# A two-layer decoder with routed experts on one core: gathering raw residual rows, a sliced router, and 32-column tiles in mixed passes

## What is computed

```
scores = sigmoid(h @ w_router)                  # 64 experts
sel = scores + router_bias
grp = sel.reshape(N, 8, 8)                      # 8 groups of 8
gscore = sum of the two largest of each group   # the best 4 groups stay
idx = the 6 largest of sel in those groups
w = scores[idx]; w = w / sum(w) * 2.5
routed = sum over idx of w * swiglu(h, w_gate_up[e], w_down[e])
out = routed + swiglu(h, shared_gate_up, shared_down)
```

## Time and profile before

| what | value |
|---|---|
| median of 3 runs | 1378.45 us (1378.06 to 1379.5) |
| the profiled execution's own time | 1383.0 us |
| its span in the profile | 1381.2 us |
| TensorE busy, matmuls | 1176.0 us, 85% of the span |
| VectorE busy | 422.5 us, 31% |
| ScalarE busy | 253.4 us, 18% |
| moved by DMA | 502.24 MB, mean 364 GB/s |
| chain that ended last | PE 46%, SP's queue 26%, DMA 18%, DVE 5% |
| TensorE's mean granted clock | 0.942 of full speed |

### The profile page before, as it was taken

How to read it: one execution, slowest core, us unless ns; L and a number is a source line. 1 busy time by engine, 2 the same in 40 slices (tenths; PEclk the granted TensorE clock), 3 DMA queues, 4 the chain that set the end, 5 groups by cost and what they waited for, 6 DMA issues and landing times.

```text
span 1381.2 us, 17034 instructions
## 1 busy us (share of the span) xinstructions
PE 1176.0 (85%) x6576; PEld 621.2 (45%) x6576; DVE 422.5 (31%) x1026; ACT 253.4 (18%) x572; POOL 0.4 (0%) x5
## 2 busy tenths in 40 slices
PE   6999788999697799769968889899969779967996
PEld 4886367525243333323227467752524333332332
DVE  1397546312111112112132577531211211211213
ACT  1112513111111101111022263311101110110100
POOL 0000000000000000000000000000000000000000
PEclk9999989999899899999988999999989989998998
DMA  9999896779999999999976705677999999999995
GB/s 348 382 407 411 352 395 248 318 277 425 423 423 424 424 424 424 424 423 423 424 297 264 251 31 186 243 323 278 425 422 424 423 423 424 424 424 423 424 424 214
DMA packets 99913, 502.24 MB, mean 364 GB/s; under 512 B 11865, under 2 KB 37366, under 8 KB 44534
## 3 DMA queue, kind: packets, MB, share of 16 engines
q1 hardware_dynamic: 99366, 500.92, 89.2%
q10 hardware_dynamic: 464, 0.20, 0.1%
HBM read 500.04 MB, written 1.05 MB: 363 GB/s over the span
## 4 chain that ended last, share of the span: by engine, by line
PE 46%; SPq 26%; DMA 18%; DVE 5%; issue 3%; ACT 2%; DVEq 0%; ACTq 0%
PE bank L707 39%; SPq L579 24%; DMA w_gu<-in_moe_w_gate_up 7%; DMA xn<-in_moe_w_gate_up 4%; DMA w_gu_x<-in_moe_w_gate_up 4%; PE bank L925 2%; PE bank L1090 2%; DMA ring<-in_ada_w 2%; PE bank L710 2%; SPq L665 2%; DMA ring<-in_a_w_o 1%; PE bank L1071 1%; SPq L639 1%; ACT p_sb L1310 1%; DVE x L1796 0%
## 5 line engine op out<-in xcount | busy, mean ns | idle before, releaser
L707 PE MATMUL bank<-w_gu,ring 128*32 128x512 f32 (+1 forms) x1024 | 356.6, 672 | 60.8 <-DMA w_gu<-in_moe_w_gate_up 55.0
L707 PEld LDWEIGHTS bank<-w_gu,ring 128*32 128x32 f32 (+1 forms) x1024 | 88.5, 132 | 214.2 <-issue 214.2
L707 PE MATMUL bank<-ring 128*32 128x512 f32 (+1 forms) x368 | 170.1, 689 | 12.1 <-DMA w_gu<-in_moe_w_gate_up 12.1
L707 PE MATMUL bank<-w_gu,hhT 128*32 128x512 f32 (+1 forms) x560 | 159.8, 604 | 0.0
L1728 DVE TENSOR_TENSOR hh<-sg,bank 128x256 f32<-128x256 f32 x44 | 27.4, 623 | 421.1 <-ACT sg L1343 421.1
L707 PE MATMUL bank<-w_gu_x,ring 128*32 128x512 f32 (+1 forms) x304 | 135.7, 630 | 22.9 <-DMA w_gu<-in_moe_w_gate_up 18.3
L1745 DVE SCALAR_TENSOR_TENSOR y_lo<-bank,w_slot,y_hi 128x512 fp32r<-128x512 f32 x88 | 62.0, 747 | 198.6 <-ACT y_hi L1233 198.6
L1343 ACT ACTIVATE sg<-bank 128x256 f32<-128x256 f32 x44 | 16.9, 385 | 499.4 <-PE bank L707 499.4
L707 PE MATMUL bank<-w_dn,ring 128*32 128x512 f32 x240 | 91.2, 735 | 18.4 <-DMA w_gu<-in_moe_w_gate_up 10.2
L707 PE MATMUL bank<-sel,h_hi 128*128 128x256 f32 x352 | 87.8, 289 | 0.0
L1233 ACT ACTIVATE y_hi<-bank,w_slot 128x512 fp32r<-128x512 f32 x88 | 55.7, 684 | 170.8 <-PE bank L707 170.8
(11 more groups left out here) (285 smaller groups left out, 1568.8 us busy)
## 6 DMA issues: line engine op xcount, KB each, us to landing
w_gu<-in_moe_w_gate_up SPq DMA_DIRECT2D x126, 1024.0 KB, 25.7
w_gu<-in_moe_w_down SPq DMA_DIRECT2D x68, 1024.0 KB, 26.2
ring<-in_ada_w SPq DMA_DIRECT2D x44, 1024.0 KB, 11.0
ring<-in_moe_w_gate_up SPq DMA_DIRECT2D x44, 1024.0 KB, 26.4
w_gu_x<-in_moe_w_gate_up SPq DMA_DIRECT2D x38, 1024.0 KB, 24.9
w_dn<-in_moe_w_gate_up SPq DMA_DIRECT2D x30, 1024.0 KB, 25.3
ring<-in_moe_w_down SPq DMA_DIRECT2D x16, 1024.0 KB, 26.0
w_dn<-in_moe_w_down SPq DMA_DIRECT2D x14, 1024.0 KB, 26.0
```

Of the source, the lines that this page charges most:

```text
L707: return nc.tensor.matmul(o, a, b, start=first, stop=last)
```

## The change

1. **Tiles.** In a pass, all tiles are now as wide as its narrowest part: the mixed passes use four tiles of 32 columns.
2. **Gather from the raw residual.** `h_hi` and `h_lo` are made in `norm` from `x` times the reciprocal root (ACT, then DVE between its two pieces of `hT`), reading x with a stride of 8 elements (`by_pk`). The 16 transposes, four copies and four subtractions in `experts` are gone. The modulation is applied when gathered rows leave PSUM: eight activations of 256 columns with bias and scale, where four of 512 stood for a pair of passes. The columns that this needs (`mod_pk`) come from `columns_pk(g)`, 16 matmuls of one column each, behind the four of groups 1, 2 and 4, and for group 5 behind layer 1's router. Three small loads fetch the bias and norm gain in that layout (`rows_pk`).
3. **Router** by slices: it starts on piece j as soon as that piece of `hT` is written.
4. **Selection** on DVE: four masked products and sums and one more operation are replaced by one; two memsets are moved ahead.
5. **Order ahead of tables**, with pieces of the shared product between the steps; `gate_up(0)` is no longer behind the tables; `gate_up(1)` is split by them.
6. **Layer 1's MoE gate** is computed after `gate_up(0)` instead of ahead of the router. The copy of the row sums of groups 3 and 5 is DVE's.
7. `dynamic_dma_scratch_size` goes from 1024 to 512.

```diff
@@ add_pass
+    tile = min(C, *[width for _, width in parts])
...
-        for s0 in range(0, width, C):
-            w = min(C, width - s0)
+        for s0 in range(0, width, tile):
+            w = min(tile, width - s0)
@@ sync
+                    for n in range(2):
+                        sp.dma_start(rows_pk[:, n, 0:2, :], t["ada_b"][n:n + 1, 3 * D:5 * D].rearrange("a (s p k) -> p (a s) k", p=P, k=KT))\
+                          .then_inc(sem("mask_in"), 16)
+                    sp.dma_start(rows_pk[:, :, 2, :], t["norm2_g"].rearrange("l (p k) -> p l k", k=KT)).then_inc(sem("mask_in"), 16)
@@ tensor
+            def columns_pk(g):
+                q0 = 2 if g in (1, 4) else 0
+                for u in range(2):
+                    for k in range(KT):
+                        last = mm(bank[7][64 * u:64 * u + 64, 16 + k:17 + k], row_of[g][:, k:k + 505:KT],
+                                  const("quarters")[:, q0 + u:q0 + u + 1], True, True)
+                return last
@@ tensor, experts
-                for j in range(4):
-                    ti, half = j // 2, j % 2
-                    for k in range(4):
-                        last = tr(bank[j][:, k * P:(k + 1) * P], hT[:, 4 * half + k, ti * P:(ti + 1) * P])
-                    last.then_inc(sem("h_ps"), 1)
...
+                if l == 1:
+                    columns_pk(5).then_inc(sem("ada_ps"), 1)
+                shared_part(0, 0, 6, 0, KT)
+                shared_part(0, 1, 6, 0, 4)
                 pe.wait_ge(sem("chosen"), l + 1)
...
+                shared_part(0, 1, 6, 4, 6)
...
                 gather_half(0, 0)
                 gather_half(0, 1, (2, 3))
+                pe.wait_ge(sem("flags"), l + 1)
...
+                shared_part(0, 1, 6, 6, KT)
+                gate_up(0)
...
+                gate_up(1, (0,))
...
+                gate_up(1, (1,))
                 middle(0)
@@ scalar, norm
-                    ada_rows(ADA_IN_WO[n // 2])
+                    nc.scalar.activation(small[:, 34:35], eps_c, ACT.Sigmoid)
+                    act.wait_ge(sem("xn_ready"), 2 * n + 2)
+                    for ti in range(NT):
+                        last = copy(h_hi[:, ti, :, :], by_pk(x[:, ti, :]), scale=small[:, 4 + ti:5 + ti])
+                    last.then_inc(sem("h_act"), 1)
@@ scalar, gathered
-                    for b in (1, 0):
-                        k = 4 * half + 2 * b
-                        last = copy(xg[l][i % 2][:, k:k + 2, :].rearrange("p k c -> p (k c)"), bank[banks[b]][:, :])
+                    for kk in range(4):
+                        k = 4 * half + kk
+                        last = nc.scalar.activation(xg[l][i % 2][:, k, :], bank[banks[kk // 2]][:, (kk % 2) * N:(kk % 2 + 1) * N],
+                                                    ACT.Identity, bias=mod_pk[:, l, 0, k:k + 1], scale=mod_pk[:, l, 1, k:k + 1])
@@ vector, norm
+                    if n != 2 and j == 0:
+                        dve.wait_ge(sem("h_act"), n // 2 + 1)
+                        for ti in range(NT):
+                            last = v.scalar_tensor_tensor(out=h_lo[:, ti, :, :], in0=by_pk(x[:, ti, :]), scalar=small[:, 4 + ti:5 + ti],
+                                                          in1=h_hi[:, ti, :, :].bitcast(F32), op0=ALU.mult, op1=ALU.subtract)
+                        last.then_inc(sem("h_dve"), 1)
```

More of the change, by code:

```diff
@@ L270, in build @@
         amp = sb("amp", [P, 5, KT])
+        rows_pk = sb("rows_pk", [P, 2, 3, KT])
+        mod_pk = sb("mod_pk", [P, 2, 2, KT])
         qk_gain = sb("qk_gain", [P, 2])
@@ L732, in ada_columns @@
                     last = mm(bank[7][:, m:m + 13:4], row_of[g][:, m * P:(m + 1) * P], const("quarters"), True, True)
+                if g in (1, 2, 4):
+                    last = columns_pk(g)
                 last.then_inc(sem("ada_ps"), 1)
@@ L899, in gather_pair, with gate_up @@
                     last.then_inc(sem(f"gath_done{l}"), 1)
-                def gate_up(p):
+                def gate_up(p, halves=(0, 1)):
                     pe.wait_ge(sem(f"xg_ready{l}"), 2 * (p // 2) + 2)
-                    if p == 0:
-                        pe.wait_ge(sem("order"), l + 1)
-                    elif p >= 2:
+                    if p >= 2:
                         pe.wait_ge(sem(f"st_ready{l}"), p)
-                    for half in range(2):
+                    for half in halves:
                         for j in positions(p):
@@ L991, in experts @@
                 last.then_inc(sem("at_ps"), 1)
-                gate_up(0)
-                gate_up(1)
                 pe.wait_ge(sem("onehot"), l + 1)
@@ L1370, in experts @@
                         act.wait_ge(sem(f"gath_done{l}"), p + 1)
-                        for b, k in ((7, 4), (4, 0)):
-                            last = copy(xg[l][0][:, k:k + 4, 0:P], bank[b][:, :].rearrange("p (k c) -> p k c", c=P))
+                        for k in range(KT):
+                            last = nc.scalar.activation(xg[l][0][:, k, 0:P], bank[4 if k < 4 else 7][:, (k % 4) * P:(k % 4 + 1) * P],
+                                                        ACT.Identity, bias=mod_pk[:, l, 0, k:k + 1], scale=mod_pk[:, l, 1, k:k + 1])
                         last.then_inc(sem(f"xg_ready{l}"), 1)
@@ L1604, in experts @@
                 big = 1e30
+                v.memset(gsc[:, :, G:G + TOPG], big)
+                link(V, v.memset(choice[:, :, E:E + 2], big))
                 dve.wait_ge(sem("score"), l + 1)
@@ L1634, in experts @@
                 v.tensor_tensor(chosen[:, :, :], left[:, :, 0:E], choice[:, :, 0:E], ALU.not_equal).then_inc(sem("chosen"), 1)
-                for j in range(4):
-                    dve.wait_ge(sem("h_act"), 4 * l + j + 1)
-                    v.tensor_tensor(interleaved(h_lo, j), in_order(bank[j]), interleaved(h_hi, j).bitcast(F32), ALU.subtract)\
-                        .then_inc(sem("h_dve"), 1)
+                if l == 1:
+                    dve.wait_ge(sem("ada_ps"), ADA_TURN[5] + 2)
+                    scale_pk(1)
                 dve.wait_ge(sem("ranks"), l + 1)
```

107 lines of the change are left out of this document (57 added, 50 removed).

## The result

| | before | changed |
|---|---|---|
| median of the runs | 1378.26 us (1376.82 to 1379.50) | 1394.16 us (1391.07 to 1397.27) |
| profiled execution | 1383.0 us, span 1381.2 | 1391.07 us, span 1389.2 |
| mean granted clock | 0.942 | 0.922 |

A forecast was written before the change was run, and what follows sets the result against it. Full-rate transfers bound the expert passes; only time when they don't run, behind PE's chain, can be shortened. 16.4 + 4.5 + 1.4 - 5.9 = 16.4 us saved, from 1378.45 to 1362.0 us, range 1354 to 1373.

The forecast's parts named there:

- Mixed tiles, 16.4 saved: Pass 2 of either expert layer: all tiles at 32 columns keep transfers fed, saving 8.2 us twice.
- Chain to the gather, layer 0, 4.5 earlier: Layer 0, norm to `middle` of pass 0: earlier logits, shorter selection and new order bring `middle` 4.5 us earlier.
- nearer to the plain copy because the new one writes contiguously: Norm on ACT: reason to price `h_hi` at 1.3 us per 1024, between ends of 1.0 and 1.86.
- Layer 1, 1.4 earlier: Layer 1's chain: 4.5 + 1.0 for gates moved, less 1.9 for their return and 2.2 for `columns_pk(5)`.
- Front, 5.9 lost: Ahead of layer 0's experts: `columns_pk` of groups 1 and 4 costs 4.4 us, `rows_pk` loads 1.5; range 2.2 to 9.
- PE runs at full clock at those places: At the `columns_pk` places: argument against a matmul costing the low-clock 0.47 us, in the slower case of chance 0.04.
- The scratch size: POOL issues no DMA: Whole kernel: the smaller `dynamic_dma_scratch_size` was listed as without effect.
- Strided reads are dear: Rival on `h_hi`, `h_lo` and `columns_pk`: 32-byte strides raise their price, only 5.6 us saved, 1373 us; chance 0.15.
- The floor of 60 cycles: `columns_pk` matmuls: a skill's minimum, 0.05 us for two instructions, would better the sum by 4.2 us; 0.14 was used.
- Slower: the price of a `columns_pk` matmul: Rival: three groups on the path eat the gain at 0.48 us a matmul; at 0.6 us, 1384 us; chance 0.04.
- signs of being wrong: `h_hi` or `h_lo` over 1.8 us, last `x_part` at 216 or beyond 226, or rate dips in passes 3 and 4.

The follow-up runs named there:

- reads without stride: Changed kernel with `h_hi` and `h_lo` reading x contiguously, gathered columns in wrong order; 1422.05 us, a time that says nothing as other experts were picked.
- repaired: Changed kernel at the addresses of before, without `columns_pk`, the modulation row copied by two small DMAs per group on ACT's queue; 1372.64 us, ratio 0.9959.
- repaired, old mixed tiles: The repaired kernel with the mixed tiles of before, one of 64 and two of 32 columns; 1386.67 us, ratio 1.0051.
- tiles and selection: Kernel before plus 32-column tiles in mixed passes, the shorter selection on DVE and norm's row copy on DVE; 1365.22 us, ratio 0.9891.
- the changed kernel at the old addresses: Changed kernel with scratch back at 1024 and the two small tiles allocated behind `w_gu_1`, so earlier tiles keep their addresses; 1384.83 us, ratio 1.0063.

## Why the prediction was wrong

The chain in stages, us from the first loads behind the last `x_part` (start of SP's four issues) to the ranks' matmuls, then to `gate_up(0)`, `middle(0)` and the end of pass 1, layer 0 / layer 1, each from the PE and SP rows of the kernel's trace:

| | ranks | `gate_up(0)` | `middle(0)` | end of pass 1 | sum |
|---|---|---|---|---|---|
| before | 19.8 / 21.6 | 11.4 / 11.4 | 15.5 / 15.5 | 16.7 / 16.8 | 63.5 / 65.2 |
| changed | 21.8 / 25.9 | 8.2 / 8.2 | 17.2 / 20.7 | 17.1 / 18.5 | 64.2 / 73.2 |
| reads without stride | 16.7 / 22.2 | 8.3 / 8.2 | 17.2 / 20.7 | 18.6 / 18.6 | 60.8 / 69.6 |
| repaired | 20.9 / 24.2 | 8.2 / 8.2 | 17.2 / 19.0 | 18.5 / 17.0 | 64.8 / 68.3 |
| repaired, old mixed tiles | 22.5 / 23.1 | 8.2 / 8.2 | 17.2 / 20.6 | 18.6 / 18.5 | 66.6 / 70.4 |
| tiles and selection | 18.0 / 18.2 | 11.4 / 11.4 | 15.5 / 15.5 | 18.3 / 16.8 | 63.2 / 61.8 |

The two repaired kernels have the same instructions up to the end of pass 1 and differ by 1.8 and 2.1 us in the sum: the granted clock behind the router's wait differs from execution to execution. The table resolves nothing smaller.

The terms from kernel to kernel, by the ratios, each with an interval of 2 to 5 us to either side, against the forecast:

| | forecast | measured |
|---|---|---|
| mixed tiles | 16.4 saved | 12.7 saved |
| the chain with the `rows_pk` loads, without any `columns_pk` | 4.5 + 1.4 + 2.2 - 1.5 = 6.6 saved | 7.0 lost |
| the four `columns_pk` | 4.4 + 2.2 = 6.6 lost | 14.3 lost |
| addresses | nothing | 7.3 lost |
| sum | 16.4 saved | 15.9 lost |

The measured column adds up to the whole by construction, since each entry is the step from one variant to the next. No single term turned the sign: 32 us lie between forecast and result, 13.6 of them in the chain, 7.7 in `columns_pk`, 7.3 in the addresses and 3.7 in the tiles.

- **Mixed tiles, 16.4 saved.** Right in mechanism and nearly in size: 13.7 alone, 12.7 within the change; the rate behind pass 1 is 396 to 406 GB/s instead of 300, short of the 423 that I took for the whole stretch.
- **Chain to the gather, layer 0, 4.5 earlier.** The order did what I said, and with contiguous reads `middle(0)` is 4.6 us earlier. The term that failed, and the step with the largest share of the miss, is the price of `h_hi` and `h_lo`: 1.3 and 1.4 taken, 2.1 and 2.0 measured. The step "nearer to the plain copy because the new one writes contiguously" was the error; the new one reads with a stride, which costs about what writing with one did (0.93 per 512). And I let the logits depend on the sum of the two only: PE now waits 2.98 us in the middle of the router, and runs at a granted clock of 0.50 behind the wait. The chain is 0.7 us later, and 3.1 in the trace of the repaired kernel with the old mixed tiles.
- **Layer 1, 1.4 earlier.** 8.0 later. Ranks +4.3: `columns_pk(5)` took 3.55 instead of 2.2, and the stride and the clock did the rest; without it, in the repaired kernel, the ranks are still 2.6 later. `middle(0)` +5.2: the tables 1.75 and the gates 1.9 stand there now, as foreseen, and 1.7 of low clock in half of `gate_up(1)` was not.
- **Front, 5.9 lost.** 8.2 in the trace, but 17 by the ratio when `columns_pk` is added alone, and 14.3 for all four within the change. Two steps failed. I priced a matmul at 0.14 us from a row whose stationary operand is contiguous, and the strided one takes 0.22; without the stride it is 0.12, so the row was a fair one for that. And I took the clock as given ("PE runs at full clock at those places"); it does ahead of them, but behind them it falls, and the product there takes 8.76 instead of 7.07 (group 1) and 15.77 instead of 14.06 (group 4).
- **"The scratch size: POOL issues no DMA", no effect.** True for the scratch and beside the point: I put the allocation of two tiles at nothing without a reason. It moves all tiles behind them, the full slices fall from 424 to 421 GB/s, and the ratios give 7.3 us.
- **The rivals.** "Strided reads are dear" was the right one in mechanism, at a chance of 0.15 and with too small a price, since it held neither clock nor addresses. The rule that I set beside it (the Trainium skill, SBUF — State Buffer, Door 1: The DMA port swizzle: accesses that go to a new line of 16 bytes pay) agrees with ACT and DVE: 2.1 against 1.09, 2.0 against 1.24. No run has a stride of less than 16 bytes, so the length of the line isn't tested. The floor of 60 cycles (the Trainium skill, TensorEngine Tiling (Array Packing), Instruction Overhead), by my estimate 0.05 us for a matmul of two instructions, is not what bounds these matmuls: they take 0.12 even without a stride. "Slower: the price of a `columns_pk` matmul" needed 0.48 us a matmul by issue alone; 17 us over 48 matmuls is 0.36, of which only 0.22 is issue. Of the signs of being wrong that I had named, one came, `h_hi` and `h_lo` at over 1.8 us; the last `x_part`, at 224, stayed below the 226. (A slip in reading that nothing hangs on: the full slices of layer 0 begin with the tenth and not behind it.)

One thing stays open in part. The traces account for 8 us, the ratios say 16, and with `columns_pk` alone it is 7.6 against 17. The variants spread more from execution to execution than before does: the nine of the changed kernel at the old addresses lie at 1382.5 to 1384.8 (five) and at 1389.5 to 1393.4 (four), the repaired one at 1368.8 to 1379.4, before beside them at 1377.0 to 1383.6. The traced executions of the changed kernel and of the strided `columns_pk` are the fastest of theirs. Two places show what such an execution can gain. The strided one reaches its first small `ada_row` product at 27.43 us, where before does at 30.43, and nothing was added ahead of that. And the first 32 instructions of the output product take 7.14 us in it and in the changed kernel, 9.97 before. The variant with reads without a stride has the same front as the changed kernel and takes 8.79 there; its first loads stand at 227.32 instead of 224.41, 11.1 us behind before. What the executions without a trace did at these places was not seen.

## What to carry to other kernels

Price an added operation with what it does to the engine's clock and to the instructions behind it; a run of many tiny matmuls on a busy PE cost more than one and a half times its issue time here (17 us for 48 at 0.22), and two small copies on ACT's queue, 1.2 us of issue, did the same work. When a change allocates a tile, keep the addresses of the others or put it last, and compare the full-rate slices of the two pages before anything else. A part of a change that needs nothing new (here a tile width) is best measured alone: it carried all of the gain.

## What was unexpected of the hardware

- Moving tiles by 320 bytes lowered the rate of large loads from 424 to 421 GB/s in every full slice, though 13 of the 17 units had kept their places; moving all tiles by 512 didn't.
- Behind 32 instructions of 64x1, on a PE without a gap, the granted clock from 100 to 104 us was 0.50 to 0.75 in each of the five traces that have them at that place, and 1.00 in the nine that don't. At a second place it fell behind the strided ones (15.77 us for 14.06) and not behind the contiguous ones (14.08).
- A strided stationary operand of 64 columns cost 0.22 us a matmul, a contiguous one 0.12.
- A copy or multiply of 1024 fp32 elements with a read stride of 32 bytes took 2.1 us on ACT and 2.0 on DVE; without it 1.09 and 1.24.
